# Moving the sums of the modulation vectors from VectorE to GpSimd

## The reference

```
cond = jax.nn.silu(c)
for layer in range(DEPTH_2):
    mod = (cond @ ada_w[layer] + ada_b[layer])[:, None, :]
    shift_m, scale_m, gate_m, shift_f, scale_f, gate_f = jnp.split(mod, 6, axis=-1)
    h = rmsnorm(x, norm_mix_g[layer]) * (1.0 + scale_m) + shift_m
    ...                                       # attention groups (layer 0) or gated delta net (layer 1)
    x = x + gate_m * mixed
    h = rmsnorm(x, norm_ffn_g[layer]) * (1.0 + scale_f) + shift_f
    x = x + gate_f * swiglu(h, ffn_w_in[layer], ffn_w_out[layer])
```

## Time and profile before

| | |
|---|---|
| median of 3 executions | 3368.31 us (3364.58 to 3371.21) |
| the profiled execution | 3371.89 us, its span 3370.6 us |
| mean granted clock of TensorE | 0.913 |
| PE busy | 2853.0 us (85% of the span) |
| DVE busy | 1257.3 us (37%) |
| ACT busy | 838.9 us (25%) |
| POOL busy | 274.3 us (8%) |

### The profile page before, as it was taken

One profiled execution on the slowest core, in us unless ns is written; L12 is line 12 of the kernel. 1 busy time (PEld: TensorE's weight loads), 2 busy tenths in 40 slices (PEclk: granted clock), 3 DMA queues, 4 the chain that ended last, 5 costly groups with the idle time before them and its releaser, 6 DMA issues. The chain is left out here.

```text
span 3370.6 us, 35541 instructions
## 1 busy us (share of the span) xinstructions
PE 2853.0 (85%) x14172; PEld 2253.0 (67%) x14172; DVE 1257.3 (37%) x2313; ACT 838.9 (25%) x1646; POOL 274.3 (8%) x492
## 2 busy tenths in 40 slices
PE   7898976779878779599898799988778778879998
PEld 5788875566555445286666678867577576657886
DVE  4433334242221111210552656434545544343333
ACT  2222221242121111110462322223212212232221
POOL 0000002310001015220000000000110120000000
PEclk9988887989988999799999899998889889989999
DMA  6222220002348994321001456322002001222322
GB/s 202 88 88 88 82 81 5 29 7 85 91 163 325 425 424 154 131 90 36 1 1 50 150 172 213 114 59 70 13 1 51 25 1 33 68 80 83 105 81 64
DMA packets 325651, 339.41 MB, mean 101 GB/s; under 512 B 19120, under 2 KB 296752, under 8 KB 313072
## 3 DMA queue, kind: packets, MB, share of 16 engines
q1 hardware_dynamic: 303280, 280.21, 25.2%
q0 software_dynamic: 22208, 56.93, 4.6%
HBM read 370.63 MB, written 16.78 MB: 115 GB/s over the span
## 5 line engine op out<-in xcount | busy, mean ns | idle before, releaser
L330 PE MATMUL bank<-sb_h_hi,sb_w_hi 128*128 128x512 f32 x1088 | 443.8, 408 | 65.9 <-DVE sb_w_lo L320 65.9
L320 DVE TENSOR_TENSOR sb_w_lo<-sb_weights,sb_w_hi 128x1024 fp32r<-128x1024 f32 x224 | 250.4, 1129 | 527.8 <-ACT sb_w_hi L314 527.5
L332 PE MATMUL bank<-sb_h_hi,sb_w_lo 128*128 128x512 f32 x1088 | 429.9, 395 | 0.0
L331 PE MATMUL bank<-sb_h_lo,sb_w_hi 128*128 128x512 f32 x1088 | 429.8, 395 | 0.0
L314 ACT CAST sb_w_hi<-sb_weights 128x1024 fp32r<-128x1024 f32 x224 | 215.6, 970 | 629.4 <-PE bank L332 572.6
L330 PEld LDWEIGHTS bank<-sb_h_hi,sb_w_hi 128*128 128x128 f32 x1088 | 207.6, 191 | 131.1 <-issue 86.8
L793 PE MATMUL bank<-sb_weights,sb_hT 128*128 128x256 f32 x960 | 236.5, 404 | 14.4 <-DVE sb_padded L1245 12.4
L331 PEld LDWEIGHTS bank<-sb_h_lo,sb_w_hi 128*128 128x128 f32 x1088 | 207.7, 191 | 48.3 <-issue 5.3
L332 PEld LDWEIGHTS bank<-sb_h_hi,sb_w_lo 128*128 128x128 f32 x1088 | 207.3, 191 | 46.1
L793 PEld LDWEIGHTS bank<-sb_weights,sb_hT 128*128 128x128 f32 x960 | 216.3, 286 | 25.9 <-issue 13.2
L330 PE MATMUL bank<-sb_hidden_hi,sb_w_hi 128*128 128x512 f32 x352 | 141.6, 402 | 12.9 <-DVE sb_hidden_lo L1494 12.9
(11 more groups left out here) (462 smaller groups left out, 4955.3 us busy)
## 6 DMA issues: line engine op xcount, KB each, us to landing
sb_weights<-ffn_w_in SPq DMA_DIRECT2D x88, 512.0 KB
sb_mod_weights<-ada_w POOLq DMA_DIRECT2D x24, 1024.0 KB, 5.9
sb_weights<-ada_w SPq DMA_DIRECT2D x24, 1024.0 KB
sb_weights<-w_in SPq DMA_DIRECT2D x16, 1024.0 KB
sb_weights<-ffn_w_out SPq DMA_DIRECT2D x32, 512.0 KB
sb_weights<-gdn_w_in SPq DMA_DIRECT2D x32, 512.0 KB
sb_expert_weights<-w_up SPq DMA_DIRECT2D x14, 1024.0 KB, 24.1
sb_expert_weights<-w_gate SPq DMA_DIRECT2D x14, 1024.0 KB, 25.2
```

The source lines that it names most:

```text
L320: dve.tensor_tensor(u.lo[:, 0:u.kt, :], u.chunk.w, u.hi[:, 0:u.kt, :].bitcast(F32), ALU.subtract).then_inc(*k.lo.one())
L330: pe.matmul(bank[:], u.hi[:, kk, :], act[0][:, kk, :], start=first and kk == 0, stop=False)
L331: pe.matmul(bank[:], u.hi[:, kk, :], act[1][:, kk, :], start=False, stop=False)
L332: mm = pe.matmul(bank[:], u.lo[:, kk, :], act[0][:, kk, :], start=False, stop=last and kk == u.kt - 1)
```

## The change

The sums move from DVE to POOL. A piece is there one product of the whole [128, 8, 256] tile with `cond`, in place, and three additions that halve it (1024, 512, 256 columns), each behind a wait for the one before it. Layer 0's pieces are no longer loaded stage by stage: POOL loads the first two, and after each sum the piece two further on. PE's turns come later: after steps 7, 12, 17, 22 of a projection, 11, 20, 29, 38 of an attention, and in the swiglu at the end of step n+4 for piece n.

```diff
 def modulation_pool(k, pieces):
     pool = k.nc.gpsimd
     for p in pieces:
-        for mark in p.chunk.prev.freed:
-            pool.wait_ge(*mark)
-        pool.dma_start(p.chunk.w, p.chunk.src).then_inc(p.chunk.slot.sem, 16)
...
+        if p.i == 0:
+            modulation_load(pool, p)
+            modulation_load(pool, pieces[1])
+            pool.wait_ge(*k.cond_ready)
+        acc, w = k.scr[8 + p.i % 2], p.chunk.w
+        pool.wait_ge(*p.chunk.ready)
+        if p.i >= 2:
+            pool.wait_ge(k.mod_turned.sem, p.i - 1)
+        pool.tensor_tensor(w, w, k.cond[:].unsqueeze(2).to_broadcast([P, KD, MOD_W]), ALU.mult
+                           ).then_inc(*k.pool_step.one())
+        for n in (4, 2):
+            pool.wait_ge(*k.pool_step.last())
+            pool.tensor_tensor(w[:, 0:n, :], w[:, 0:n, :], w[:, n:2 * n, :], ALU.add).then_inc(*k.pool_step.one())
+        pool.wait_ge(*k.pool_step.last())
+        pool.tensor_tensor(acc[:, 0:MOD_W], w[:, 0, :], w[:, 1, :], ALU.add).then_inc(*k.pool_summed.one())
+        p.chunk.freed = [k.pool_summed.last()]
+        if p.later:
+            modulation_load(pool, p.later)
...
 def modulation_pe(k, p):
     pe = k.nc.tensor
-    pe.wait_ge(k.mod_summed.sem, p.i + 1)
+    pe.wait_ge(k.pool_summed.sem, p.i + 1)
...
+    all_pieces = [Piece(k, 0, n) for n in range(24)]
+    for p, after in zip(all_pieces, all_pieces[2:] + [None, None]):
+        p.later = after
...
-        on_dve = {2 + 6 * n: p for n, p in enumerate(pieces[:4])}
-        on_pe = {5 + 6 * n: p for n, p in enumerate(pieces[:4])}
+        pieces = all_pieces[8 * g:8 * g + 8]
+        on_pe = {7 + 5 * n: p for n, p in enumerate(pieces[:4])}
...
-        on_dve = {3 + 8 * n: p for n, p in enumerate(pieces[4:])}
-        on_pe = {7 + 8 * n: p for n, p in enumerate(pieces[4:])}
+        on_pe = {11 + 9 * n: p for n, p in enumerate(pieces[4:])}
...
-    swiglu_pe(k, steps, h, hid, {s + 2: p for s, p in enumerate(pieces)})
+    swiglu_pe(k, steps, h, hid, {s + 4: p for s, p in enumerate(pieces)})
     swiglu_act(k, steps, hid)
-    swiglu_dve(k, steps, hid, lambda j: k.mod[:, layer, 5, j:j + 1], dict(enumerate(pieces)))
+    swiglu_dve(k, steps, hid, lambda j: k.mod[:, layer, 5, j:j + 1])
+    modulation_pool(k, pieces)
     load_weights_sp(k, order)
```

More of the change, by code:

```diff
@@ L207, in __init__ @@
         self.added = Count(self, "DVE", "added")
-        self.mod_summed = Count(self, "DVE", "mod_summed")
         self.padded_odd = Count(self, "DVE", "padded_odd")
@@ L221, in __init__ @@
         self.roped = Count(self, "POOL", "roped")
+        self.pool_summed = Count(self, "POOL", "pool_summed")
         self.pool_rows = Count(self, "POOL", "pool_rows")
@@ L550, in attention_act, with attention_dve @@
                      ).then_inc(*k.mixed_in.one())
-def attention_dve(k, jobs, padded, normalise, out=None, mod=()):
+def attention_dve(k, jobs, padded, normalise, out=None):
     dve = k.nc.vector
@@ L591, in attention_dve @@
                                   den.unsqueeze(2).to_broadcast([P, H, HD]), ALU.mult).then_inc(*k.evacuated.one())
-        if s in mod:
-            modulation_dve(k, mod[s])
 MOD_W = 256
@@ L604, in __init__, with modulation_load @@
         self.layer, self.c = layer, c
-        self.i = k.mod_pieces
+        self.i, self.later = k.mod_pieces, None
         k.mod_pieces += 1
         self.chunk = k.mod_weights.plan(k.io["ada_w_2"][layer], c * MOD_W, MOD_W)
+def modulation_load(engine, p):
+    for mark in p.chunk.prev.freed:
+        engine.wait_ge(*mark)
+    engine.dma_start(p.chunk.w, p.chunk.src).then_inc(p.chunk.slot.sem, 16)
 def modulation_pool(k, pieces):
@@ L828, in dilated_project_act, with dilated_project_dve @@
                            scale=columns(k.col[("qdil", "kdil")[part]], g)).then_inc(*k.gained.one())
-def dilated_project_dve(k, other, mod):
+def dilated_project_dve(k, other):
     dve = k.nc.vector
@@ L858, in dilated @@
                   for part in range(3) for half in range(2)]
-        pieces = [Piece(k, 0, 8 * g + n) for n in range(8)]
-        on_dve = {2 + 6 * n: p for n, p in enumerate(pieces[:4])}
-        on_pe = {5 + 6 * n: p for n, p in enumerate(pieces[:4])}
+        pieces = all_pieces[8 * g:8 * g + 8]
+        on_pe = {7 + 5 * n: p for n, p in enumerate(pieces[:4])}
         dilated_project_pe(k, g, chunks, on_pe)
         dilated_project_act(k, g, q, kt, v)
-        dilated_project_dve(k, other if g == 0 else iter(()), on_dve)
+        dilated_project_dve(k, other if g == 0 else iter(()))
         if g == 0:
@@ L882, in dilated @@
                                 k.negmax[:, g, i, h:h + 1], k.dens[:, g, i, h:h + 1]))
-        on_dve = {3 + 8 * n: p for n, p in enumerate(pieces[4:])}
-        on_pe = {7 + 8 * n: p for n, p in enumerate(pieces[4:])}
+        on_pe = {11 + 9 * n: p for n, p in enumerate(pieces[4:])}
         attention_pe(k, jobs, True, False, on_pe)
         attention_act(k, jobs, (q, k.padded), False)
-        attention_dve(k, jobs, (q, k.padded), False, outs[g], on_dve)
+        attention_dve(k, jobs, (q, k.padded), False, outs[g])
         modulation_pool(k, pieces[4:])
@@ L1476, in swiglu_act, with swiglu_dve @@
             pairs += 1
-def swiglu_dve(k, steps, hid, gate, mod):
+def swiglu_dve(k, steps, hid, gate):
     dve = k.nc.vector
```

## The result

| | before | after |
|---|---|---|
| median | 3367.96 us (4 runs, 3364.58 to 3371.21) | 3429.6 us (4 runs, 3428.42 to 3430.33) |
| span of the profiled execution | 3370.6 us | 3427.8 us |
| mean granted clock of TensorE | 0.913 | 0.909 |

After is slower: the ratio is 1.0183, with a 95% interval of 1.0165 to 1.02, some 62 us by the medians and 57.2 us by the two profiles. The forecast was 3420 us. I read the profile of after in the order of before: windows, waits, then the timeline inside a wait.

A forecast was written before the change was run, and what follows sets the result against it. PE was taken to bound the swiglu, while DVE's sums delay PE in the attentions. A swiglu loss of 123 us less an attention gain of 71 gives +52 on 3368.3, so 3420 us, range 3380 to 3465.

The forecast's parts named there:

- T: Time of one piece's product and three additions on POOL: 8.2 us, upper end 9.1.
- The choice of the slope: POOL's product: 1.67 ns a column (3.60 us) taken as the nearer form; the other slope gives 4.49 us.
- The gain of the attentions: Three dilated attentions get shorter: 25.4 + 23.6 + 22.4 = 71 us, bounds 50 and 80.
- Groups 1 and 2: Their attentions: POOL's four pieces in a row bound them at 36.8 us against PE's 34.4; taken as 39.
- the 9.2 in the sum: POOL's chain in an attention, T plus 0.88 us of load issue: a piece each 9.2 us.
- the 2 us allowed for the clock: Attentions of groups 1 and 2: 2 us for a slower clock after short waits, within the 39.
- Group 0: First attention, bound by PE: 8 x 0.78 + 24 x 1.31 + 3.5 of drain + 4 = 45 us.
- the 1.31 us for a step with 256 keys: Group 0's attention: PE's time for each of 24 steps, read as the distance of two L470.
- The loss of the swiglu: Late turns delay weight loads, so PE stands before steps 6 to 26: 123 us lost, bounds 90 and 150.
- That the loads stay ahead (3297): Rival 1: swiglu loads stay ahead as now, only the 71 us gain remains, 3297 us; chance 0.06.
- That the engines don't wait for each other (3387): Rival 2: VectorE and GpSimd don't wait out each other's instructions; loss 90, gain 71, 3387 us; chance 0.17.
- That POOL bounds the attentions harder (3458): Rival 3: T of 9.1 or delayed DVE copies; gain 50, loss 140, 3458 us; chance 0.17.

The follow-up runs named there:

- e8: e1 with both halves of the padded queries copied by ScalarE, so VectorE has no SBUF-to-SBUF copy in the attentions: 3308.92 us, ratio 0.9814.
- e1: The changed kernel, but in the swiglu PE turns piece n at the end of step n+2, not n+4: 3305.06 us, ratio 0.9804.
- e6: The changed kernel (turn at n+4), but the swiglu's lo part is a second ScalarE cast, no VectorE difference; low part's values left out: 3397.97 us.

## Why the prediction was right, and where it was off

**The piece on POOL.** Its rows in after, the timeline of the first piece:

```profile
40.26 3.60 POOL L626 TENSOR_TENSOR sb_mod_weights<-sb_mod_weights,sb_cond 128x2048 f32<-128x2048 f32 x1 [3.94 <-DMA sb_mod_weights<-ada_w]
...
43.94 3.70 POOL L630 TENSOR_TENSOR sb_mod_weights<-sb_mod_weights 128x1024 f32<-128x1024 f32 x2
...
47.72 0.73 POOL L632 TENSOR_TENSOR sb_scratch<-sb_mod_weights 128x256 f32<-128x256 f32 x1
```

3.60, 3.70 and 0.73, with some 0.08 at each wait: T is 8.19 us, predicted 8.2. The straight line through the rows of the near forms held to four times their length. The choice of the slope was what mattered, since the other would have given 9.1. The Trainium skill (GPSIMD Engine Reference, Performance versus the Vector engine) has 4497 ns for an add of 2048 columns, and the measured 3.60 us of this product with one number for 256 columns is below it. Beside DVE's work T grows: the piece in the timeline above, from 1870.69 to 1880.59, took 9.9 us. The forecast had nothing for it; it costs nothing here, for that piece's slot is not the one that is late.

**The gain of the attentions** is 70.2 us against 71, but its terms were off and cancelled, so that the total came out this close is luck. Groups 1 and 2 took 38.6 and 36.5 us for 39 each. In group 1 the four L626 begin at 274.98, 284.70, 294.75 and 304.27, 9.5 to 10.1 us apart for the 9.2 in the sum, and PE waits 3.1 us for the fourth sum; of the 2 us allowed for the clock there was little need. Group 0 took 49.1 us for 45. There PE is busy for 46.9 of them, so it is no wait, as I first took it to be, and e8, which removed the copies, had little to remove there. The step that failed is the 1.31 us for a step with 256 keys: it was read from two steps at the start of that stretch, before the second tile's transposes and values came in from the pipeline. In the timeline of PE in after the first distance is of such a step, the second of a full one:

```profile
138.79 0.65 PE L470 MATMUL bank<-sb_arena,sb_padded 128*128 128x256 f32 x2
...
140.10 0.65 PE L470 MATMUL bank<-sb_arena,sb_padded 128*128 128x256 f32 x2
...
143.38 0.65 PE L470 MATMUL bank<-sb_arena,sb_padded 128*128 128x256 f32 x2
...
144.91 0.65 PE L470 MATMUL bank<-sb_arena,sb_padded 128*128 128x256 f32 x2
```

1.31 and 1.53 us. 24 times the difference is 5.3 us, which makes the sum 50, for 49.1 measured.

**The loss of the swiglu** is 126.3 us against 123. By steps: stands of 9.04 and five of 8.76 us before the six pair steps (predicted 9.1), 7.31 and three of 7.40 before steps 14, 16, 18 and 20 (7.3), 18.30 before step 12 (17.9), and none new after step 27, each at the step named. The waits sum up to 52.8 + 29.5 (47.6 less the 18.1 at the start) + 18.3 less the 3.1 that were there before, 97.5 us. The other 28.8 are clock, 2.6 a stand for 11 stands where I took 2.4: PE's busy time in the windows, 405.49 for 376.70 us with the same 1680 matmuls, differs by just this. The sum was also short of clock in one place, since step 12 stands in it with 15 us, hardly more than 17.9 less 3.1. What a stand costs in clock can be seen in a step itself: the pair step that began at 1879.31 ended with a turn at 1892.72, so 13.4 us to the turn, where a pair step without a stand takes 10.9 (the distance of 11.4 less 0.5 for the turn itself).

**The other forecasts of the profile.** L481's longest wait is 2.6 us, not under 2. POOL's turn waits, SP's waits for POOL and ACT's casts released by transfers are all there. The swiglu's window was to be near 508 us and is 511.7.

**The rivals.** That the loads stay ahead (3297) failed as such, but e1 is its world: with the turn at n+2 they do stay ahead, and the time is 3305. Of the 8 us between them 5 are the swiglu's, which that rival left as it was. That the engines don't wait for each other (3387) is refuted by L320, which takes 3.10 and 3.35 us beside POOL for 1.13, and e6 shows about its size: 3398 with that waiting taken out of the weights. I had 33 us for it, and e6 gives 31, by an edit that also lengthens ACT's work. That POOL bounds the attentions harder (3458) failed on T; the other half of that rival, the copies that wait for POOL, is there, but with 9.9 us of PE's waits, and the gain is 70 and not 50. That 3420 is 9.6 us under the median has two parts. By the profiles the terms are +126.3 and -69.2, together 57 where I had 52: 5 us are the sum's, above all the 3 of the loss. The other 4 are between the profiles (57.2) and the medians (61.6), and with an interval of the ratio that is worth 3424 to 3435 us they are not told apart from the spread.

## What to carry to other kernels

When work moves to a slower engine, ask first which slot, tile or bank it gives back and who is queued for it in order: here a consumer placed two steps later turned 25 us of slack into a chain of 20 us that has one step of 11 to hide in, for 126 us, and moving it back by a single line gave all but some 5 of them back. Work out such a chain from its release to its use and compare it with the steps it spans: as long as it fits it costs nothing, and beyond that every round pays the difference. And before curing a wait, look at the next-latest engine: the pads' wait was real, but behind it stood POOL's own line, and only taking pieces from POOL's full stretch to its empty one gained.

## What the runs showed of the hardware

In these traces an instruction of DVE with two inputs from SBUF waits out a whole instruction of POOL: L320 with 128x512 takes 0.69 us on average in the swiglu of before and 3.89 in e1, where it ends 0.5 us after POOL's product. DVE's SBUF-to-SBUF copy with a single input does so too: L521 with 64x512 takes 0.42 us before and 3.43 beside the same product. The forecast had counted on the first and had the copy only in a rival. The waiting is mutual: POOL's two additions take 3.70 us alone and 5.41 between two L320. The rule of the Trainium skill (SBUF — State Buffer, SBUF: two separate sides) has VectorE and GpSimd take turns at one port pair, a whole instruction each, and names among VectorE's forms those with two inputs from SBUF and, under Who interferes with whom, copies that can run in a mode with both ports. The trace agrees that both kinds wait. ACT's cast isn't touched by it: 1.04 us beside POOL's product in e6. So what DVE loses in these two forms is set by the length of POOL's single instruction, not by POOL's share of the time.

The clock gave a second number. The 11 stands of 7 to 18 us in the swiglu cost some 2.6 us each beyond their own length, worked out above; 28.8 of 126.3 us is over a fifth of the loss.
